# A depthwise convolution as matmuls with diagonal weights on TensorE in place of a loop on GpSimd, in a two-layer encoder trunk

## What is computed

```python
z = _rms(h, norm1_g[l]) @ w_in[l]
za, zr, zc = split(z)                     # attention, RWKV-7, convolution columns
h = h + concat([_attention_group(za), _rwkv_group(zr), _conv_group(zc)]) @ w_out[l]
h = h + _peer(_rms(h, norm2_g[l]), ...)   # 16 of 16384 experts for each of 8 heads and token

def _conv_group(z, conv_w, conv_b, ln_g, ln_b):      # CONV_CH = 256, CONV_K = 31
    u = z[..., :CONV_CH] * sigmoid(z[..., CONV_CH:])
    u = causal_depthwise_conv(u, conv_w) + conv_b     # per channel: sum over k of w[k] * u[t - 30 + k]
    return silu(_layernorm(u, ln_g, ln_b))
```

## Time and profile before

| what | value |
|---|---|
| median of 3 runs | 2781.23 us (2776.55 to 2783.92) |
| span of the profiled execution | 2772.8 us |
| time of the profiled execution beside its span | not given |
| busy: PE, PEld, DVE, ACT, POOL | 90%, 87%, 65%, 41%, 62% of the span |
| mean granted clock of TensorE | 0.938 |
| DMA | 320.20 MB, 115 GB/s |

### The profile page before, as it was taken

The page is one execution under the profiler, slowest core; times in us unless marked ns, Lnnn a source line. Parts: engine busy times, 40 slices in busy tenths (PEclk is TensorE's granted clock), DMA queues, the critical chain, the costliest instruction groups (busy, mean ns, idle before and its releaser), DMA issues.

```text
span 2772.8 us, 53248 instructions
## 1 busy us (share of the span) xinstructions
PE 2496.0 (90%) x19057; PEld 2413.2 (87%) x19057; DVE 1805.6 (65%) x2889; ACT 1149.3 (41%) x1675; POOL 1713.1 (62%) x789
## 2 busy tenths in 40 slices
PE   7787799989999899999988777999999999998887
PEld 7776799989998799999978777989999999998887
DVE  2764329977676677756655744189089987776665
ACT  3512356645544133333334322466645443333332
POOL 4791368866665355566646961678766665555665
PEclk9857899999999899999999658999999999999999
DMA  4100144534343233344434000445444433333443
GB/s 150 54 1 1 61 159 162 165 121 136 130 134 114 69 121 121 121 136 144 144 114 137 1 0 28 153 147 173 159 136 137 136 129 124 125 125 125 151 147 126
DMA packets 88232, 320.20 MB, mean 115 GB/s; under 512 B 9696, under 2 KB 10976, under 8 KB 87776
## 3 DMA queue, kind: packets, MB, share of 16 engines
q1 hardware_dynamic: 88160, 319.24, 34.9%
HBM read 318.15 MB, written 1.05 MB: 115 GB/s over the span
## 4 chain that ended last, share of the span: by engine, by line
PE 38%; issue 23%; POOL 21%; DVE 11%; DMA 5%; ACT 1%; DVEq 1%; POOLq 0%; ACTq 0%; SPq 0%
PE ps L797 38%; POOL w_lo L504 13%; POOL arena L525 5%; DMA w<-v_c 4%; DVE x_hi L1552 4%; POOL arena L534 3%; DVE onehots_j L1532 3%; DVE onehots_i L1536 2%; DVE onehots_i L1538 2%; ACT x_hi L780 1%; DVE arena L1546 0%; DVE h L1612 0%; DMA w<-w_c 0%; DMA arena<-lora_c 0%; DVEq L1538 0%
## 5 line engine op out<-in xcount | busy, mean ns | idle before, releaser
L504 POOL TENSOR_TENSOR w_lo<-w,w_hi 128x1024 fp32r<-128x1024 f32 x596 | 1487.0, 2501 | 1032.7 <-ACT w_hi L582 1031.7
L797 PE MATMUL ps<-x_hi,w_hi 128*128 128x256 f32 (+3 forms) x7072 | 1614.8, 290 | 93.0 <-DVE x_hi L1552 49.5
L797 PE MATMUL ps<-x_hi,w_lo 128*128 128x272 f32 (+3 forms) x4896 | 1398.3, 286 | 0.0
L797 PEld LDWEIGHTS ps<-x_hi,w_hi 128*128 128x128 f32 x7072 | 1199.5, 191 | 113.8 <-POOL w_lo L504 87.6
L797 PEld LDWEIGHTS ps<-x_hi,w_lo 128*128 128x128 f32 x4896 | 933.1, 191 | 0.0
L582 ACT CAST w_hi<-w 128x1024 fp32r<-128x1024 f32 x596 | 624.3, 1048 | 674.4 <-DMA w<-v_c 614.4
L797 PE MATMUL ps<-x_lo,w_hi 128*128 128x272 f32 (+1 forms) x2720 | 779.9, 287 | 0.0
L797 PEld LDWEIGHTS ps<-x_lo,w_hi 128*128 128x128 f32 x2720 | 519.4, 191 | 0.2
L1552 DVE TENSOR_TENSOR x_hi<-arena,x_hi 128x272 fp32r<-128x272 f32 (+1 forms) x256 | 349.7, 1366 | 177.5 <-ACT x_hi L780 168.2
L797 PE MATMUL ps<-arena 128*128 128x64 f32 (+9 forms) x1448 | 261.7, 354 | 77.5 <-ACT arena L613 16.0
L797 PEld LDWEIGHTS ps<-arena 128*128 128x128 f32 (+6 forms) x1448 | 234.5, 243 | 101.1 <-issue 27.7
(11 more groups left out here) (153 smaller groups left out, 1321.7 us busy)
## 6 DMA issues: line engine op xcount, KB each, us to landing
w<-u_c SPq DMA_DIRECT2D x256, 512.0 KB, 3.3
w<-v_c SPq DMA_DIRECT2D x256, 512.0 KB, 3.3
w<-w_c SPq DMA_DIRECT2D x84, 512.0 KB, 3.3
arena<-keys_c SPq DMA_DIRECT2D x2, 1024.0 KB, 6.4
arena<-mix_c SPq DMA_DIRECT2D x2, 792.0 KB, 7.0
h<-h SPq DMA_DIRECT2D x1, 1088.0 KB, 5.1
out<-h SPq DMA_DIRECT2D x1, 1024.0 KB, 4.7
arena<-lora_c SPq DMA_DIRECT2D x2, 256.0 KB, 7.3
```

The source lines that it names most:

```text
L504: g.tensor_tensor(wlo_t[:, slot], wraw_t[:, slot], whi_t[:, slot].bitcast(F32), ALU.subtract).then_inc(s_lo, 1)
L797: return nc.tensor.matmul(out_, lhsT, rhs, start=start, stop=stop, skip_group_check=True)
```

## The change

The 31 taps of each of the two groups of 128 channels become 31 fp32 matmuls of 128x128 by 128x272, which accumulate in one PSUM bank: the stationary operand is a diagonal matrix of the tap's 128 weights, the moving one is `cu` shifted by the tap. Group 0 accumulates in bank 7, group 1 in bank 0.

- ACT makes the 62 diagonals (`diagonals`): the identity scaled by a column of weights, three behind each of the tiles 0 to 11, five behind each later one. They lie in parts of the arena that are free until later. The gate's two sigmoids move ahead of the wait for the low-rank products.
- POOL makes `cu` after the low half of tile 13 and then goes on with the low halves; its loop is gone.
- PE makes group 0 (`conv(0, ...)`) in fives behind tiles 12 to 17, the last time six; group 1 in the place of the 48 warm matmuls (12), behind each of 5 chunks of transposes (2 each) and of 5 chunks of gram products (2 each, 1 behind the last).
- ACT copies each group's sum to `cacc` with the bias. PE waits for the first copy ahead of the attention's squares and for the second ahead of the inverse; the wait at L1065 is gone.
- The attention's squares leave bank 0 alone, in seven pieces instead of six.

The diff, without the naming of the arena's parts and the new semaphores:

```diff
--- before.py
+++ after.py
@@ -118,7 +118,9 @@
 
 V_TILES = (("z", 0, P, (0, 0)), ("z", P, 16, (0, 1)), ("vcat", 0, P, (1, 0)), ("vcat", P, 80, (1, 1)))
 
-Q2_AT = [(1, 0, 0, T), (2, 0, 0, T), (7, 0, 0, T), (0, 0, 0, T), (1, T, 0, 512 - T), (2, T, 512 - T, 2 * T - 512)]
+REST = 2 * T - 512
+Q2_AT = [(0, 1, 0, 0, T), (1, 2, 0, 0, T), (2, 7, 0, 0, T), (3, 1, T, 0, 512 - T), (4, 2, T, 0, 512 - T),
+         (3, 7, T, 512 - T, REST), (4, 7, T + REST, 512 - T, REST)]
 
 
 WARM = dict(prepare=48, norm=30)
...
@@ -347,6 +353,14 @@
         topi_u = topi.bitcast(U32).rearrange("p (h s k) -> p h s k", h=PH, s=2)
         fi_u = fi.bitcast(U32)
         fa_u = fa.bitcast(U32)
+
+        taps = [vkb_t[:, k * P:(k + 1) * P] for k in range(NCH * 3 * 2)]
+        taps.append(cat_t[:, 16 * P:17 * P])
+        taps += [cat_t[:, k * P:(k + 1) * P] for k in range(16)]
+        taps += [ctmp_t[:, k * P:(k + 1) * P] for k in range(4)]
+        taps += [yT_t[:, k * P:(k + 1) * P] for k in range(5)]
+        taps += [sq_t[:, (5 * T) + k * P:(5 * T) + (k + 1) * P] for k in range(6)]
+        assert len(taps) == 2 * CONV_K
 
         def mix(name, parts=P):
             a, n = MIX[name]
...
@@ -514,26 +531,13 @@
                     low(l, n)
 
             for l in range(DEPTH):
-                lows(l, 0 if l == 0 else AHEAD, NZ + AHEAD)
+                lows(l, 0 if l == 0 else AHEAD, 14)
 
                 pool.wait_ge(s_cg, 2 * (l + 1))
-                link(g.memset(cu[:, :, 0:CPAD], 0.0))
-                link(g.tensor_tensor(cu[:, :, CPAD:CPAD + T], z[:, ZCU:ZCU + 2, 1:T + 1], cacc[:, :, :], ALU.mult))
-                for k in range(CONV_K):
-                    for j in range(2):
-                        dst = cacc if k == 0 else ctmp
-                        ins = g.tensor_scalar(dst[:, j, :], cu[:, j, k:k + T], vcol(l, "conv_w", j * CONV_K + k),
-                                              vcol(l, "conv_b", j) if k == 0 else None, ALU.mult,
-                                              *((ALU.add,) if k == 0 else ()))
-                        if j == 0:
-                            ins.then_inc(s_gl, 1)
-                            link.n += 1
-                        else:
-                            link(ins)
-                    if k:
-                        ins = g.tensor_tensor(cacc[:, :, :], cacc[:, :, :], ctmp[:, :, :], ALU.add)
-                        link(ins) if k < CONV_K - 1 else ins.then_inc(s_conv, 1)
-                lows(l, NZ + AHEAD, NW)
+                g.memset(cu[:, :, 0:CPAD], 0.0).then_inc(s_cui, 1)
+                g.tensor_tensor(cu[:, :, CPAD:CPAD + T], z[:, ZCU:ZCU + 2, 1:T + 1], cacc[:, :, :],
+                                ALU.mult).then_inc(s_cui, 1)
+                lows(l, 14, NW)
                 if l < DEPTH - 1:
                     for n in range(AHEAD):
                         low(l + 1, n)
@@ -617,8 +621,8 @@
 
                 yield
                 act.wait_ge(s_q2s, l + 1)
-                root(qn, [(qn[:, min(c, 4), t0:t0 + n], ps[:, bank, at:at + n])
-                           for c, (bank, at, t0, n) in enumerate(Q2_AT)], 1.0 / HD,
+                root(qn, [(qn[:, c, t0:t0 + n], ps[:, bank, at:at + n])
+                           for c, bank, at, t0, n in Q2_AT], 1.0 / HD,
                       res("norm_eps")).then_inc(s_qs, 1)
                 for _ in range(8):
                     yield
@@ -659,12 +663,21 @@
                         high(0, n)
                 norm_scale(l, 0)
                 x_high(l, 0, xn)
+                def diagonals(k0, k1):
+
+                    for k in range(k0, min(k1, 2 * CONV_K)):
+                        nc.scalar.activation(taps[k], ident, ACT.Copy, scale=vcol(l, "conv_w", k)).then_inc(s_cvd, 1)
+
                 for n in range(12):
                     evacuate(l, n, z[:, n, 1:T + 1], T)
+                    diagonals(3 * n, 3 * n + 3)
 
                 act.wait_ge(s_zs, 2 * l + 2)
                 nc.scalar.activation(th[0:HD, :], zs[0:HD, 6, :], ACT.Tanh).then_inc(s_th, 1)
                 nc.scalar.activation(sg[:, :], zs[:, 7, :], ACT.Sigmoid).then_inc(s_sg, 1)
+                act.wait_ge(s_ea, l * (NZ + NQ) + 12)
+                for j in range(2):
+                    nc.scalar.activation(cacc[:, j, :], z[:, ZCG + j, 1:T + 1], ACT.Sigmoid).then_inc(s_cg, 1)
                 act.wait_ge(s_lora, 6 * l + 6)
                 for j in range(2):
                     nc.scalar.activation(ea[:, j, :], ps[:, 3 + j, 0:T], ACT.Sigmoid,
@@ -675,10 +688,12 @@
                 for j in range(2):
                     nc.scalar.copy(gg[:, j, :], ps[:, 7 if j == 0 else 0, 0:T]).then_inc(s_ag, 1)
 
-                for j in range(2):
-                    nc.scalar.activation(cacc[:, j, :], z[:, ZCG + j, 1:T + 1], ACT.Sigmoid).then_inc(s_cg, 1)
                 for n in range(12, NZ):
                     evacuate(l, n, z[:, n, 1:T + 1], T)
+                    diagonals(36 + 5 * (n - 12), 41 + 5 * (n - 12))
+                act.wait_ge(s_cvp, 2 * l + 1)
+                nc.scalar.activation(cacc[:, 0, :], ps[:, 7, 0:T], ACT.Identity,
+                                     bias=vcol(l, "conv_b", 0)).then_inc(s_conv, 1)
                 act.wait_ge(s_var, l + 1)
                 root(t2[:, :, :]).then_inc(s_rs, 1)
 
@@ -704,6 +719,9 @@
                 after(steps)
 
                 act.wait_ge(s_grc, NCH * (l + 1))
+                act.wait_ge(s_cvp, 2 * l + 2)
+                nc.scalar.activation(cacc[:, 1, :], ps[:, 0, 0:T], ACT.Identity,
+                                     bias=vcol(l, "conv_b", 1)).then_inc(s_conv, 1)
                 blocks(g0_d, gram[:, :, :, 0, :].rearrange("p c j t -> p j c t")).then_inc(s_g0, 1)
 
                 for b in range(len(LEVELS) - 1):
@@ -846,8 +864,9 @@
 
                 pe.wait_ge(s_q2, l + 1)
                 pe.wait_ge(s_ea, l * (NZ + NQ) + NZ)
-                for c, (bank, at, t0, n) in enumerate(Q2_AT):
-                    last = mm(ps[:, bank, at:at + n], blk, sq[:, min(c, 4), t0:t0 + n], True, True)
+                pe.wait_ge(s_conv, 2 * l + 1)
+                for c, bank, at, t0, n in Q2_AT:
+                    last = mm(ps[:, bank, at:at + n], blk, sq[:, c, t0:t0 + n], True, True)
                 last.then_inc(s_q2s, 1)
                 yield
                 for _ in range(7):
@@ -921,6 +940,18 @@
 
                         pe.wait_ge(s_ea, l * (NZ + NQ) + n - 1)
                     project(l, n)
+
+                def conv(j, k0, k1):
+
+                    if k0 == 0 and j == 0:
+                        pe.wait_ge(s_ag, 6 * l + 6)
+                        pe.wait_ge(s_cui, 2 * l + 2)
+                    for k in range(k0, min(k1, CONV_K)):
+                        pe.wait_ge(s_cvd, 2 * CONV_K * l + j * CONV_K + k + 1)
+                        last = mm(ps[:, 7 - 7 * j, 0:T], taps[j * CONV_K + k], cu[:, j, k:k + T], k == 0,
+                                  k == CONV_K - 1)
+                        if k == CONV_K - 1:
+                            last.then_inc(s_cvp, 1)
 
                 for n in range(NZ):
                     if n == 12:
@@ -937,6 +968,8 @@
                             mm(ps[:, 7 if j == 0 else 0, 0:T], lora[:, 1, j * P:(j + 1) * P], sg[:, :],
                                True, True).then_inc(s_lora, 1)
                     proj_in(n)
+                    if n >= 12:
+                        conv(0, 5 * (n - 12), 5 * (n - 12) + (5 if n < NZ - 1 else 6))
 
 
                 pe.wait_ge(s_ag, 6 * l + 6)
@@ -951,7 +984,7 @@
                 last.then_inc(s_pd, 1)
                 steps = attention(l)
                 pe.wait_ge(s_ea, l * (NZ + NQ) + NZ)
-                warm(WARM["prepare"], 1)
+                conv(1, 0, 12)
 
                 asked()
                 pe.wait_ge(s_dg, 3 * (l + 1))
@@ -965,6 +998,7 @@
                                                           (2 * (m % 2) + j) * P:(2 * (m % 2) + j + 1) * P],
                                                        src[:, j, c, :], ident)
                     last.then_inc(s_tm, 1)
+                    conv(1, 12 + 2 * c, 14 + 2 * c)
 
                 after(steps)
                 pe.wait_ge(s_tmc, (l + 1) * NCH)
@@ -980,11 +1014,13 @@
                                a[:, j, c, :], alrh[:, :, j, w], True, True)
                         last = mm(ps[:, 3 + j, c * CHUNK:(c + 1) * CHUNK], al_d[:, j, c, :], be[:, j, w], True, True)
                     last.then_inc(s_gram, 1)
+                    conv(1, 22 + 2 * c, 24 + 2 * c if c < NCH - 1 else CONV_K)
                     if c >= 3:
                         after(steps)
 
 
                 pe.wait_ge(s_qs, l + 1)
+                pe.wait_ge(s_conv, 2 * l + 2)
                 nlev = len(LEVELS) - 1
                 for b in range(nlev):
                     for j in range(2):
@@ -1062,7 +1098,6 @@
                 for _ in steps:
                     pass
 
-                pe.wait_ge(s_conv, l + 1)
                 for k in range(2):
```

15 lines of the change are left out of this document (11 added, 4 removed).

## The result

| | before | after |
|---|---|---|
| median (runs, from to) | 2778.89 us (4, 2766.67 to 2783.92) | 2815.07 us (4, 2801.0 to 2833.71) |
| ratio, 95% interval | 1 | 1.0154 [1.0089, 1.0219] |
| profiled execution: time, span | not given, 2772.8 us | 2833.71 us, 2831.7 us |
| granted clock, mean | 0.938 | 0.935 |

The change makes the kernel slower by 36 us. The forecast was +22, to 2803, and its range ended at 2818: the sign was right and the price too low. The median lies just inside the range; the ratio, put on the 2781.23 us from which the forecast started, gives 2824 us, above it. In the profiled execution the spans differ by 58.9 us. Where that is, is read in three steps: the rows that answer to those of before, the two mixers as wholes, and the stage that the prediction called unchanged.

A forecast was written before the change was run, and what follows sets the result against it. It took PE's projection tiles up to 96.35 us, then DVE, to bound the mixer. Terms of +19.6 up to the inverse less 8.2 gave +11.4, the second layer +10.9, together +22 on 2781.23: 2803 us, range 2786 to 2818.

The forecast's parts named there:

- 31 products among the tiles, +14.1, and +1.1 for the transition: Projection tiles 12 to 17: group 0's products lengthen PE's path by 14.1 us, six starts behind fp32 matmuls by 1.1.
- DVE's slack, -3.8: At DVE's L1342: it came 3.8 us after PE's first norm product, so that much of the delay is absorbed.
- Contention in the chain, -2.3: DVE's chain ahead of the transposes: L1346, L1354 and L1358 get shorter without POOL's loop, 2.3 us in all.
- The gap, 6 us, then half clock, +2.6, and ten products, +3.5: PE idles 6 us ahead of the transposes, restarts at half clock (+2.6 us); ten products among the transposes add 3.5.
- Rival 1: Transposes and their products stay at half clock throughout: +5.3 us a layer, 2814 us; chance 0.15.
- Gram stage, +3.6: Gram products on PE: the stage is packed, and eight convolution products ahead of its last chunk add 3.6 us.
- Relief in the inverse, -8.2: The recurrence's inverse: DVE's instructions, no longer slowed by POOL's loop, save 8.2 us in the first layer.
- rival 2: PE and ACT are last in the inverse, so the relief misses the path: +16 us, 2819; chance 0.1.
- Rival 4: Clock stays full from the inverse on, its PE-bound half takes half: -23 us a layer, 2757; chance 0.07.
- Rival 5: Projection tiles wait for weights anyway, so products don't delay DVE: +2 us or so; counted within the 0.13 for same.
- Sum of the mixers, +22: Both mixers together: first layer +11.4 us, second +10.9, put on the median of 2781.23 us.
- Nothing changed after the mixer: All stages behind the mixer, the expert output stage included, were to stay as they were: 0 us.

The follow-up runs named there:

- the memset: The kernel before and the changed kernel, each with a memset in place of DVE's subtraction that makes `act_lo`: 2708.27 and 2732.09 us.
- either wait: Kernel before and change, POOL waiting for `act_lo` of two tiles earlier: 2771.06, 2792.23 us; or one tile earlier from the first tile without gates: 2718.16, 2728.89.
- the half version: The changed kernel with only group 0's products on PE, in its wait for DVE, and group 1 in POOL's loop: 2773.51 us, ratio 1.0004.

## Why the prediction was right or wrong

- **The loop is off the path, its removal gives only the relief.** Right. Without it the kernel gains 0.54%.
- **31 products among the tiles, +14.1, and +1.1 for the transition.** 0.46 us each, as forecast, so 14.2; tile 12 gave 0.5 back, which leaves 13.7. The transition is 0, its lower bound. The +0.8 for the diagonals is 0.9: tile 12 starts 46.8 us after the layer's memset where it was 46.0.
- **DVE's slack, -3.8.** Right: L1377 is 10.9 us later against the memset, 3.7 less than 0.9 + 13.7. DVE waits 16.74 us for PE.
- **Contention in the chain, -2.3.** Measured 13.76 to 11.26 us from L1342 or L1377 to L1358 or L1393: -2.5.
- **The gap, 6 us, then half clock, +2.6, and ten products, +3.5.** The gap is 5.65. From the first transpose to the fifth pair of products it is 9.97 us, with that pair (0.92) 10.9, against 4.37 up to the gram stage before: +6.5 for a forecast of 6.1. Rival 1 falls: the clock was full again after two rounds of transposes and eight product records, and did not stay low through all five. The two rounds ran at 0.50; what came behind them, from 129.7 us on, at 1.00. By the Trainium skill, TensorE: Matmul & The Clock Gate, "Part 4: PE-mode transpose", transposes don't count as busy for the clock. The rise at 129.7 came with transposes and products mixed, so it neither shows nor refutes that; no run here has transposes alone.
- **Gram stage, +3.6.** It is 13.1 us long where it was 9.3, +3.8. The first inverse step, L1411, comes 18.6 us later against the memset than L1376 of before, forecast 19.6.
- **Relief in the inverse, -8.2.** L1261 and L1267 take 16.5 us against 23.0. The first inverse, from the last gram result to the copy behind it, is 94.6 us long where it was 101.8: -7.2, so rival 2 falls for this layer; the run with the loop cut, whose mixers are hardly shorter, says that such a gain need not reach the mixer's end. Behind the inverse this mixer loses 4 us more for which the sum has no term (18.6 - 7.2 against 15.6). Rival 4 falls: from 148.3 to 233.0 us the granted clock is 0.51. Rival 5, with its tiles that wait for weights, falls with the 13.7 us. The collision rows say the same of the rule that was weighed: the Trainium skill, SBUF — State Buffer, "Who interferes with whom", has a tensor_tensor with both inputs in SBUF blocked as a whole by a reading GpSimd instruction. The trace agrees: 0.43 us become 2.57 beside POOL's 2.60, and 0.4 when DVE is first.
- **Sum of the mixers, +22, put on 2781.23 us.** The later medians of before, 2773.77 to 2779.82, make that base 1 to 7 us too high. Measured by the same two rows of each layer in four pairs of traces (the change, with the memset, and with either wait, each against its own kernel before): 26.1, 21.0, 15.7 and 27.2 us, 22.5 in the mean, or 20.6 with the second trace of the change (+12.8). The sum is right in the mean; that it agrees to 2 us is luck where single pairs lie between 12.8 and 27.2.
- **"Nothing changed after the mixer"** is the step that failed. It was costed at nothing without naming what holds it there. The order of L1552 and POOL's L504 in a stage 550 us later is not fixed by any wait, and the kernel before was near the edge: in its own stretch with gates POOL's low half starts 0.1 to 0.4 us behind `act_lo` in 29 of 64 tiles, and is never under way when `act_lo` starts. (Its mean of 1366 ns for `act_lo`, and the 3.8% of L1552 in the chain, come nearly all from the tiles without gates, where the bad order is the rule.) In the traces of the four kernels or executions with all 62 products and nothing done to the order the stretch with gates took 311.8, 287.0, 301.1 and 283.7 us; in four traces without them, or with 31, 272.1, 271.5, 271.5 and, with the loop cut, 287.3. That removing the collision brings the difference from 36.6 to 23.8 and 21.2 us is shown: some 13 to 15 us of the change's price are this step.

Why the changed kernel meets the bad order more often is visible in part. In all eight of these traces SyncE issues one weight load 10.4 us after the stretch's first `act_lo`, and ACT rounds that tile as soon as it has landed; here before, then after, and the instruction queue's share of the DMA in after from 2295.2 to 2299.2 us (packets, MB):

```profile
2279.01 1.05 ACT L582 CAST w_hi<-w 128x1024 fp32r<-128x1024 f32 x1 [2.98 <-DMA w<-v_c]
```

```profile
2299.48 1.05 ACT L586 CAST w_hi<-w 128x1024 fp32r<-128x1024 f32 x1 [3.83 <-DMA w<-v_c]
```

```profile
q8 instruction: 1, 0.02, 1.4%
```

That is 3.3 us from issue to ACT before and 4.2 after, and 4 us later POOL starts its first collision, with L1573. A 16 KB packet of the instruction queue, which loads the program's code, falls into this load 10.2 to 11.4 us after the first `act_lo` in six traces (the change twice, with group 0 moved, with the memset, and with either wait), and there the load takes 3.7 to 4.2 us. In the other ten, of the kernel before in all its versions, the half version, the one without products and the one with 24 more warm matmuls, the packet comes earlier or later, and the load takes 3.1 to 3.3. So what visibly differs at this point is when code is loaded. No run moves that packet alone, so that it starts the slip is not shown; and in two traces (the loop cut, 24 warm matmuls) the order slips only 160 and 190 us into the stretch, for a reason that stays open.

## What to carry to other kernels

Before work is moved onto the engine that bounds a stage, look for the stretch where that engine itself waits: the same 31 products cost 14 us among tiles that PE runs without a gap and nothing in PE's wait for DVE. And where instructions of two engines block each other in a pipelined loop with no wait between them, as DVE's and POOL's did here, their order can turn with an edit far away, and a forecast of "nothing changes there" needs a reason. An instruction whose mean in the profile is three times its shortest like (1366 ns against 413) is the sign, and one semaphore wait that fixes the order was worth more here (2.1%) than the change that was studied.

## What the hardware showed that was not expected

- The same stage with the same instructions takes 4.25 us a tile, and 4.87 in the mean when `act_lo` is blocked in 12 of 64 tiles; 0.3 us in POOL's start decide it. A block also costs clock: 0.57 granted over 4 us behind a wait of 1.45 us.
- One load of 512 KB took 3.7 to 4.2 us in place of 3.1 to 3.3 in the six traces where a 16 KB packet of code fell into it.
- A wait one tile too early removed the surplus and most of the scatter and gained the kernel before nothing in the median (2771.06 us); one tile later it had 2718.16.
- An fp32 matmul of 272 columns with new weights each time took 0.46 us beside fp32r tiles, and entering or leaving fp32 cost PE nothing measurable.
